# A residual add split between two engines, and the fourth weight unit's split moved behind it

## The reference

```python
for i in range(DEPTH):
    g = norm_gains[i]
    h = h + 0.5 * _rmsnorm(_swiglu(_rmsnorm(h, g[0, 0]), ffn_w_in[i, 0], ffn_w_out[i, 0]), g[0, 1])
    u = _rmsnorm(h, g[1, 0])
    m = mixer(u)          # stick-breaking attention, latent attention or RWKV-7, by i % 3
    h = h + _rmsnorm(m, g[1, 1])
    h = h + 0.5 * _rmsnorm(_swiglu(_rmsnorm(h, g[2, 0]), ffn_w_in[i, 1], ffn_w_out[i, 1]), g[2, 1])
return h[:, N_META:]
```

## Time and profile before

| | |
|---|---|
| median of 3 runs | 2467.89 us |
| the profiled execution | 2467.77 us, span 2466.0 us |
| TensorE busy | 2335.2 us (95%) |
| POOL busy | 1816.6 us (74%) |
| DVE busy | 1475.7 us (60%) |
| ACT busy | 1019.0 us (41%) |
| TensorE's granted clock, mean | 0.977 of 2.4 GHz |

### The profile page before, as it was taken

The page is one execution under the profiler, slowest core; times in us unless marked ns, Lnnn a source line. Parts: engine busy times, 40 slices in busy tenths (PEclk is TensorE's granted clock), DMA queues, the critical chain, the costliest instruction groups (busy, mean ns, idle before and its releaser), DMA issues.

```text
span 2466.0 us, 53538 instructions
## 1 busy us (share of the span) xinstructions
PE 2335.2 (95%) x20654; PEld 2259.9 (92%) x20664; DVE 1475.7 (60%) x1834; ACT 1019.0 (41%) x1513; POOL 1816.6 (74%) x853
## 2 busy tenths in 40 slices
PE   7999999999999789999999689989999999999998
PEld 7999989999998789999999578988999999998997
DVE  6972148935963336963981866636982893335982
ACT  4344344344343434344343444324343434444342
POOL 5887737887886607887888796837888788746886
PEclk9999999999999989999999689999999999999999
DMA  5554524554563304564554232013554455433553
GB/s 185 172 193 139 180 65 141 173 201 128 171 196 121 122 10 145 170 198 126 171 189 157 79 112 94 5 37 106 174 185 166 149 180 190 141 108 105 176 187 112
DMA packets 89949, 348.83 MB, mean 141 GB/s; under 512 B 9968, under 2 KB 11760, under 8 KB 89712
## 3 DMA queue, kind: packets, MB, share of 16 engines
q1 hardware_dynamic: 89840, 347.31, 44.1%
HBM read 346.22 MB, written 1.05 MB: 141 GB/s over the span
## 4 chain that ended last, share of the span: by engine, by line
PE 46%; DVE 21%; issue 16%; POOL 8%; ACT 6%; DVEq 1%; DMA 0%; ACTq 0%; SPq 0%; POOLq 0%
PE bank L296 11%; PE bank L298 11%; PE bank L297 11%; DVE hid_hi L1483 8%; DVE hid L1481 6%; POOL w_lo L1263 6%; PE bank L625 3%; ACT sg L978 3%; DVE gs L1424 3%; PE bank L359 2%; DVE hid_lo L1485 1%; PE bank L360 1%; PE bank L361 1%; ACT w_hi L882 1%; POOL h L1276 1%
## 5 line engine op out<-in xcount | busy, mean ns | idle before, releaser
L1263 POOL TENSOR_TENSOR w_lo<-raw,w_hi 128x1024 fp32r<-128x1024 f32 (+2 forms) x608 | 1607.9, 2669 | 568.5 <-ACT w_hi L882 547.2
L296 PE MATMUL bank<-x_hi,w_hi 128*128 128x272 f32 (+1 forms) x3380 | 995.8, 295 | 41.2 <-POOL x_lo L1289 14.9
L298 PE MATMUL bank<-x_hi,w_lo 128*128 128x272 f32 (+1 forms) x3380 | 981.6, 290 | 0.0
L297 PE MATMUL bank<-x_lo,w_hi 128*128 128x272 f32 (+1 forms) x3380 | 978.0, 289 | 0.0
L882 ACT ACTIVATE w_hi<-raw 128x1024 fp32r<-128x1024 f32 (+2 forms) x608 | 660.7, 1115 | 233.8 <-PE bank L298 214.4
L296 PEld LDWEIGHTS bank<-x_hi,w_hi 128*128 128x128 f32 x3380 | 643.2, 190 | 57.8 <-issue 33.7
L297 PEld LDWEIGHTS bank<-x_lo,w_hi 128*128 128x128 f32 x3380 | 644.9, 191 | 0.2
L298 PEld LDWEIGHTS bank<-x_hi,w_lo 128*128 128x128 f32 x3380 | 643.8, 190 | 0.0
L1485 DVE TENSOR_TENSOR hid_lo<-hid,hid_hi 128x272 f32 (+3 forms) x176 | 423.1, 2404 | 20.2
L296 PE MATMUL bank<-hid_hi,w_hi 128*128 128x272 f32 (+1 forms) x1408 | 405.2, 288 | 3.0 <-POOL w_lo L1263 2.9
L298 PE MATMUL bank<-hid_hi,w_lo 128*128 128x272 f32 (+1 forms) x1408 | 403.4, 287 | 0.0
(11 more groups left out here) (277 smaller groups left out, 2325.1 us busy)
## 6 DMA issues: line engine op xcount, KB each, us to landing
raw<-in_ffn_in SPq DMA_DIRECT2D x352, 512.0 KB, 3.5
raw<-in_ffn_out SPq DMA_DIRECT2D x128, 704.0 KB, 4.0
raw<-in_sb_in SPq DMA_DIRECT2D x48, 512.0 KB, 3.6
raw<-in_rw_in SPq DMA_DIRECT2D x24, 512.0 KB, 3.3
raw<-in_sb_out SPq DMA_DIRECT2D x16, 512.0 KB, 3.5
raw<-in_mla_out SPq DMA_DIRECT2D x8, 512.0 KB, 3.3
raw<-in_rw_lora SPq DMA_DIRECT2D x8, 512.0 KB, 4.6
raw<-in_rw_out SPq DMA_DIRECT2D x8, 512.0 KB, 3.3
```

The source lines that it names most:

```text
L296: nc.tensor.matmul(o, wh, xh[:, k, cols()], start=start, stop=False)
L297: nc.tensor.matmul(o, wh, xl[:, k, cols()], start=False, stop=False)
L298: last = nc.tensor.matmul(o, wl, xh[:, k, cols()], start=False, stop=stop)
L1263: nc.gpsimd.tensor_tensor(w_lo[:, s, w], raw[:, s, w], w_hi[:, s, w], ALU.subtract).then_inc(lo_ready, 1)
```

## The change

1. The fourth unit (unit 3) of the next section is split behind the norm's factor on ACT and behind the adds on POOL, instead of before. The section to the latent attention (`mla_in`) is excepted.
2. Tile 0's add is done by DVE right behind its scaling. POOL adds tile 1 alone, then tiles 2 and 3, 4 and 5, 6 and 7 in one instruction each.
3. ACT squares two tiles of `h` in one instruction, behind the second's `x_hi`.
4. TensorE's paced part waits for `x_hi` alone, does the four matmuls of units 0 and 1 that need only it, and then waits for `x_lo` for the other two.
5. FILL goes from 17 to 10.

```diff
-FILL = 17
+FILL = 10
+        def fourth_unit_late(sec):
+            after = following[sec.name_key]
+            return after is not None and after.name != "mla_in"
...
 first_round, TensorE
-                paced, early = [], DT_ // 2 if behind_norm else 0
-                for k in range(DT_):
-                    paced += [(0, k), (1, k)] + ([(2, k // 2)] if early and k % 2 else [])
...
+                for k in range(DT_):
+                    if behind_norm:
+                        n["gained"] += 1
+                        pe.wait_ge(hg_hi_ready, n["gained"])
+                    else:
+                        pe.wait_ge(x_ready, base + k + 1)
+                    for s in (0, 1):
+                        o, wh, wl = w_parts(s, k)
+                        nc.tensor.matmul(o, wh, x_hi[:, k, c], start=(k == 0), stop=False)
+                        nc.tensor.matmul(o, wl, x_hi[:, k, c], start=False, stop=False)
+                    if early and k % 2:
+                        block_of_unit(2, k // 2)
+                    if behind_norm:
+                        pe.wait_ge(x_ready, base + k + 1)
+                    for s in (0, 1):
+                        o, wh, wl = w_parts(s, k)
+                        last = nc.tensor.matmul(o, wh, x_lo[:, k, c], start=False, stop=(k == DT_ - 1))
...
 gained, ACT
-                    if not first:
-                        nc.scalar.activation(m[:, k, cols()], h[:, k, cols()], ACT.Square).then_inc(hsq_ready, 1)
+                    if not first and k % 2:
+                        nc.scalar.activation(m[:, k - 1:k + 1, cols()], h[:, k - 1:k + 1, cols()], ACT.Square).then_inc(hsq_ready, 2)
...
 norm_out, ACT (squares_of leaves the unit's split out of its old place)
                 inverse_root(bank[4], 4, D, half)
+                if fourth_unit_late(sec):
+                    split_hi(following[sec.name_key], 0, 3)
...
 add_residual, POOL (output_section leaves the unit's split out of its old place)
-                for k in range(DT_):
-                    n["apply"] += 1
+                for k, count in ((1, 1), (2, 2), (4, 2), (6, 2)):
+                    n["apply"] += count
                     pool.wait_ge(apply_ready, n["apply"])
-                    nc.gpsimd.tensor_tensor(h[:, k, c], h[:, k, c], m[:, k, c], ALU.add).then_inc(h_ready, 1)
+                    nc.gpsimd.tensor_tensor(h[:, k:k + count, c], h[:, k:k + count, c], m[:, k:k + count, c], ALU.add).then_inc(h_ready, count)
+                if fourth_unit_late(sec):
+                    split_lo(following[sec.name_key], 0, 3)
...
 last_product, DVE
+                    if k == 0:
+                        steps.link(scaled)
+                        nc.vector.tensor_tensor(h[:, 0, cols()], h[:, 0, cols()], m[:, 0, cols()], ALU.add).then_inc(h_ready, 1)
+                    else:
+                        scaled.then_inc(apply_ready, 1)
                     if then and k >= LAG:
                         low_part(*then, k - LAG)
```

More of the change, by code:

```diff
@@ L345, in first_round @@
                 n["x"] += DT_
-                paced, early = [], DT_ // 2 if behind_norm else 0
-                for k in range(DT_):
-                    paced += [(0, k), (1, k)] + ([(2, k // 2)] if early and k % 2 else [])
[L349 to L352, removed]
-                    if k == 0:
[L354 to L361, removed]
+                early, c = DT_ // 2 if behind_norm else 0, cols()
@@ new lines, in first_round, with unit_begins, block_of_unit @@
+                w_parts = lambda s, k: (bank[s][:, c], w_hi[:, s, P * k:P * k + P], w_lo[:, s, P * k:P * k + P])
+                def unit_begins(s):
+                    pe.wait_ge(lo_ready, sec.start + s + 1)
+                    pe.wait_ge(bank_free[s], uses[s] + 1)
+                def block_of_unit(s, k):
+                    if k == 0:
+                        unit_begins(s)
+                    o, wh, wl = w_parts(s, k)
+                    nc.tensor.matmul(o, wh, x_hi[:, k, c], start=(k == 0), stop=False)
+                    nc.tensor.matmul(o, wh, x_lo[:, k, c], start=False, stop=False)
+                    last = nc.tensor.matmul(o, wl, x_hi[:, k, c], start=False, stop=(k == DT_ - 1))
@@ L362, in first_round @@
                     if k == DT_ - 1:
                         last.then_inc(unit_used, 1)
+                unit_begins(0)
+                unit_begins(1)
+                for k in range(DT_):
[6 more added lines that the diff above has]
+                        o, wh, wl = w_parts(s, k)
+                        nc.tensor.matmul(o, wh, x_hi[:, k, c], start=(k == 0), stop=False)
+                        nc.tensor.matmul(o, wl, x_hi[:, k, c], start=False, stop=False)
[4 more added lines that the diff above has]
+                    for s in (0, 1):
+                        o, wh, wl = w_parts(s, k)
+                        last = nc.tensor.matmul(o, wh, x_lo[:, k, c], start=False, stop=(k == DT_ - 1))
+                        if k == DT_ - 1:
+                            last.then_inc(unit_used, 1)
@@ L365, in whole @@
+                for at, (s, k) in enumerate([(2, k) for k in range(early, DT_)] + [(3, k) for k in range(DT_)]):
+                    if at == SUM_AFTER and behind_norm:
+                        input_sum(sum_cut)
+                    block_of_unit(s, k)
             def whole(s, j):
@@ L940, in input_root, with norm_out @@
                 inverse_root(xr, 5, D)
-            def norm_out(half):
+            def norm_out(sec, half):
                 n["norm"] += 1
@@ L959, in body @@
                         square(bank[2 * t if two else t][:, cols()], base + t, base + per * i + t)
-                        ahead(last)
+                        if not (fourth_unit_late(sec) and last == 3 and isinstance(i, int) and i == sec.iters - 1):
+                            ahead(last)
                 rounds(act, sec, body, split_hi)
@@ L1361, in time_mixing @@
                     split_lo(sec_out, 1, s)
-                for s in range(RING):
+                for s in range(3):
                     split_lo(following[sec_out.name_key], 0, s)
+                add_residual(sec_out)
             for s in range(RING):
@@ L1458, in last_product @@
                 for k in range(DT_):
[L1459 to L1460 removed]
+                    scaled = nc.vector.scalar_tensor_tensor(m[:, k, cols()], m[:, k, cols()], gain(layer, sub, 1, k), bank[4][:, cols()],
+                                                            ALU.mult, ALU.mult)
+                    if k == 0:
[3 more added lines that the diff above has]
+                        scaled.then_inc(apply_ready, 1)
                     if then and k >= LAG:
```

36 lines of the change are left out of this document (20 added, 16 removed).

## The result

The changed kernel takes 2492.71 us (median of 5 runs, 2491.32 to 2500.12), the kernel before 2467.89 (5 runs): ratio 1.0107, 95% interval [1.0093, 1.0122]. That is 25 us slower where 12 were forecast, and outside the range of 2463 to 2489.

The account below looks back on a forecast made before the run. TensorE's standing still at 12 boundaries behind output projections was taken as what the change could move; +10.7 (seven boundaries), +1.1, +0.4, +1.2, -1.25 and -0.2 made +11.9, so 2467.8 became 2479.7 us, range 2463 to 2489.

Parts of the forecast that it names:

- TensorE starts at 225.7 instead of 227.60: First boundary: TensorE begins with four high-part matmuls once x_hi 0 is made, a win of at most 1.9 us.
- Tile 0 on DVE is free: First boundary: DVE's add of tile 0 takes 0.44 us with no POOL work beside it.
- Pairs 1.33 long, starts 2.32 apart: POOL's adds at a boundary: 1.33 us a pair, a turn of two tiles 2.32 where two single adds took 1.86.
- x_lo 6 held by the split to 235.38: First boundary: DVE's x_lo of tile 6 starts about 233.2, during POOL's moved split, and ends 0.30 behind it.
- +1.53 a boundary: Each of seven boundaries with 272 columns grows by 1.53 us, +10.7 together.
- the sum: All forecast terms over the boundaries and the end added up: +11.9 us, giving 2479.7 us.
- The following sections give nothing back: there TensorE's own pace is the limit: Sections behind the boundaries: no change, since waits for POOL are small there.
- To the time mixing the squares start earlier, -1.25: Boundary at 1358.22 us, without x_lo: squares start at 1356.47 instead of 1357.71, saving 1.25 us.
- the gap lies nearer the one that was harmless: TensorE's gap of about 1.7 us before x_lo 6: nearer 1.44, which kept the clock, than 3.82, which halved it.
- rival 3: TensorE's clock falls to half behind the gap, 2.8 us at each of nine boundaries, +25, so 2505 us; chance 0.06.

Follow-up runs that it names:

- e17: The kernel before with one part of the change, tile 0's add on DVE and the other seven on POOL one by one; 2464.9 us, ratio 1.0000.
- e13: The kernel before with only the fourth unit's split moved behind the adds and the factor; 2480.76 us, ratio 1.0054.
- e14: The kernel before with only POOL's adds of tiles 2 and 3, 4 and 5, 6 and 7 made in pairs; 2480.13 us, ratio 1.0058.
- e12: The changed kernel, nothing altered, run again for a second profile; 2491.42 us (2 runs), ratio 1.0097.
- e5: The changed kernel with 17 fillers instead of 10; 2490.75 us, ratio 1.0097.
- e10: The changed kernel with 168 waits on a long-set semaphore (84 instructions) added on TensorE ahead of the time mixing; 2493.29 us, ratio 1.0108.
- e4: The kernel before with 10 fillers instead of 17 and nothing else; 2477.81 us, ratio 1.0037.
- e8: The changed kernel with the moved split and the pairs taken back, and 17 fillers instead of 10; 2483.27 us, ratio 1.0070.
- e18: The kernel before with high parts first and one early block of unit 2 moved behind the last low products; 2471.78 us, ratio 1.0032.
- e1: The changed kernel with the moved split taken back; 2479.08 us, ratio 1.0057.
- e3: The changed kernel with both the moved split and the pairs taken back; 2480.37 us, ratio 1.0056.
- e9: The kernel before with 344 waits on a long-set semaphore (172 instructions) added on TensorE ahead of the time mixing; 2484.4 us, ratio 1.0071.

## Why the prediction was wrong in size

- *TensorE starts at 225.7 instead of 227.60*: right. Against the scaling it started 1.67 us behind it instead of 3.47.
- *Tile 0 on DVE is free*: right (0.44, no POOL work beside it), since the split was away; e17 shows it held where it wasn't.
- *Pairs 1.33 long, starts 2.32 apart*: the length was 1.48, the turn 2.33. *x_lo 6 held by the split to 235.38*: it took 2.24, a gap of 1.51 before it. *+1.53 a boundary*: +1.65. So the mechanism at a boundary came as forecast. e13 and e14 add what the sum hid: either edit alone brings the loss. The Trainium skill (GPSIMD Engine Reference, section 8, Key points), which the prediction cites, names contention between GpSimd and DVE instructions with two SBUF inputs, and all of these rows agree. That section names no price; here a held instruction waited for the rest of the other engine's (2.24 for 0.50 at the split).
- *The following sections give nothing back: there TensorE's own pace is the limit*: wrong by 1.8 us. The wait for `w_lo` at L301 is 18.9 us where it was 15.0 at L296, and 0.5 of the 1.8 is in the very first section, where TensorE waits 1.3 instead of 0.7 for DVE's `gs`.
- *To the time mixing the squares start earlier, -1.25*: they did start 1.27 earlier, but the tiles behind come in pairs, and TensorE waits between:

```profile
1362.05 0.72 PE L405 MATMUL bank<-sq,consts 128*128 128x272 f32 x2 [2.55 <-ACT sq L917]
1363.31 0.77 PE L405 MATMUL bank<-sq,consts 128*128 128x272 f32 x2 [0.53 <-ACT sq L917]
1364.76 5.89 PE L405 MATMUL bank<-sq,consts 128*128 128x272 f32 x12 [0.68 <-ACT sq L917]
1375.74 0.56 PE L301 MATMUL bank<-x_hi,w_hi 128*128 128x272 f32 x1 [5.10 <-POOL x_lo L1336]
```

  From the square sum (1358.13) to the first product it is 17.61 us; before it was 17.49. Only e12 shows 1.0 of the gain.
- **The step that failed most is the clock.** The sum took it at nothing ("the gap lies nearer the one that was harmless"), and rival 3 took it at all nine boundaries, at 2.8 us each. A gap of 1.51 is harmless at most places and not at some. At 2256 us, first profile, TensorE and its window; then one of e12:

```profile
2285.02 0.50 PE L386 MATMUL bank<-x_lo,w_hi 128*128 128x256 f32 x2 [1.51 <-DVE x_lo L1452]
2285.47 0.41 PE L379 MATMUL bank<-x_hi,w_lo 128*128 128x256 f32 x1
```

```profile
2271.69:2290.08 18.39, 15.77 (x95) 0.91 0.25 81
```

```profile
1151.97:1171.07 19.10, 16.38 (x94) 0.91 0.17 56
2267.22:2284.09 16.87, 14.25 (x95) 1.00 0.28 91
```

  The same boundary takes 18.39 at a clock of 0.91 and 16.87 at 1.00. One, two and one of the nine were hit in the three profiles, at 1.5 us each; none of the kernel before. e5 and e10, which have the same gaps, were hit at three and at one, so it is 8 of 45. At the boundary to the latent attention, which the forecast took without the clock too, it fell in all three: its mean there is 0.82, 0.73 and 0.81, before 1.00, 0.89 and 1.00.

The sum of what the profiles show is then +19.1 against +11.9: 0.9 for the ordinary boundaries' size, 0.5 for the one of them that lost the clock (1.5 in one of three), 2.4 for the three other boundaries, 1.8 for the sections, 0.8 for the two mixers together with 1.25 that didn't come, less 0.5. The clock's part in this is at least 2.0: the 0.5, and 1.5 of the 2.4 (two hits at 2115 and one at 2256, over three profiles).

**What stays open.** The medians differ by 25, not 19: the three profiled executions of the changed kernel (2492.71, 2487.01 and 2484.94 us) lie in the lower part of its 11 (median 2492.7, up to 2500.1), those of the kernel before (2467.77, 2469.38, 2470.18) in the upper part of its 90 (median 2466.5). Over all executions the medians are 26 apart, 7 more than in the profiles. Each execution lists its mean granted clock: 0.9788 on average before, 0.9759 after. The profiled ones lie 0.0018 below that average before and 0.0018 above it after. Within one kernel 0.001 goes with 1.1 us (before) to 1.4 us (after), so this accounts for 4 to 5 of the 7 us. That the clock is lower because of the gaps at the boundaries is likely by what e4 shows, but the executions without a profile don't tell where they lost it, and the last 2 to 3 us have no name. The squares in pairs were never tested alone. What sets the number of short gaps in the time mixing wasn't found either.

## What to carry to other kernels

Where POOL and DVE both work from SBUF, an edit is priced by who meets whom, not by the instructions saved: list the long instructions of each (here 2.4 us splits) and the short ones on the path (0.44 to 0.50), and keep them apart; e13, e8 and e18 took 0.8 to 1.8 us more a boundary than the kernel before when a short instruction began 0.07 to 0.6 us behind a long one. An engine that is released earlier starts its next long instruction earlier, and that may be the one that holds the path. Profile the same kernel twice or three times before a difference in a section that isn't touched is explained: here 10 us of it were between two profiles of one kernel.

## What had not been expected of the hardware

- A DVE instruction with two SBUF operands that began just behind the start of a POOL split ended about 0.3 behind it: 2.24, 2.50, 2.60 and 2.62 us for 0.44 to 0.50.
- The granted clock fell to one half for a stretch after a gap of 1.51 at some boundaries and not at others of the same shape, and after gaps of 2.38 at four of seven. So the price of a gap is a chance, not a number. In the changed kernel and in e4 a fall cost 1.3 to 1.5 us at an ordinary boundary, in e1 0.2 (16.9 for 16.7), and in e3 nothing.
- The latent attention went from 136.0 to 142.6 us over all kernels as its mean clock went from 0.95 to 0.89, with no instruction changed.
- A wait on a semaphore that was long set wasn't free on TensorE: 172 such instructions (344 waits) pushed the next work back by 14.1 us, although the engine had 3.8 us of idle time there. The row of e9 shows 18.11 us in which TensorE waited for nothing that the profile shows (`issue`). In its weight loads this gap is 18.5 us, and 8.7 with the 84 of e10, so 0.10 to 0.11 us for each such instruction.

```profile
1369.89 6.98 PE L376 MATMUL bank<-sq,consts 128*128 128x272 f32 x16 [18.11 <-issue]
```
